# Attention over turned probabilities with the values as weights, and a turned gate, in block 2 of a two-block network

## The reference, cut to what matters

```python
hx = rms_norm(xs, norm_g) * (1 + scale_x) + shift_x
px = split_cols(hx @ w_in + b_in)
ya_x = conv_module(*px[0:3], ...)                     # 31 taps, 512 channels
yb_x, yb_c = gla_branch(px[3:9], pc[3:9], ...)        # 4 heads, chunks of 64 tokens
yc_x, yc_c = attn_branch(px[9:13], pc[9:13], ...)
xs = xs + gate_x * (merge of sigmoid(p13)*ya, sigmoid(p14)*yb, sigmoid(p15)*yc) @ w_out

def gqa_attend(q, k, v):          # 8 query heads, 2 key heads, 64 columns a head
    s = einsum('bqkgd,bskd->bkgqs', q, k) * 64 ** -0.5
    p = softmax(s, axis=-1)
    return einsum('bkgqs,bskd->bqkgd', p, v)
# attn_branch: y = (gqa_attend(...) * silu(gate)) @ w_o; latent queries see context and latent keys
# gla: o_t = q_t S_t, S_t = diag(a_t) S_{t-1} + k_t^T v_t, forward and backward; y = (rms_norm(o) * silu(gate)) @ w_o
```

## Time and profile before

| what | value |
|---|---|
| median of 3 runs | 1383.57 us (1382.19 to 1385.09) |
| the profiled execution's own time | 1383.59 us |
| its span | 1382.3 us |
| mean granted clock | 0.965 |
| TensorE busy | 1310.0 us, 95% |
| VectorE busy | 874.7 us, 63% |
| ScalarE busy | 592.0 us, 43% |
| GpSimd busy | 283.6 us, 21% |
| bytes moved | 168.18 MB |

### The profile page before, as it was taken

One profiled execution on the slowest core, in us unless ns is written; L12 is line 12 of the kernel. 1 busy time (PEld: TensorE's weight loads), 2 busy tenths in 40 slices (PEclk: granted clock), 3 DMA queues, 4 the chain that ended last, 5 costly groups with the idle time before them and its releaser, 6 DMA issues.

```text
span 1382.3 us, 19655 instructions
## 1 busy us (share of the span) xinstructions
PE 1310.0 (95%) x7838; PEld 1057.4 (77%) x7838; DVE 874.7 (63%) x1514; ACT 592.0 (43%) x985; POOL 283.6 (21%) x225
## 2 busy tenths in 40 slices
PE   7999987999979899997999999999999998899998
PEld 5777776777757777776677788888898877579997
DVE  4795766685577643488998542233776677745555
ACT  3444533344453454322433552243563554336543
POOL 0110012210033321136200011111452141300222
PEclk9999998999999999999999999999999998879999
DMA  7683465363433511112111122222653332204453
GB/s 252 224 268 134 151 244 181 126 242 138 145 114 99 162 55 60 46 62 77 61 50 57 61 62 91 92 92 92 200 166 97 107 107 77 76 31 138 131 180 117
DMA packets 49142, 168.18 MB, mean 122 GB/s; under 512 B 5844, under 2 KB 7060, under 8 KB 48794
## 3 DMA queue, kind: packets, MB, share of 16 engines
q1 hardware_dynamic: 49050, 166.92, 36.5%
HBM read 165.85 MB, written 1.05 MB: 121 GB/s over the span
## 4 chain that ended last, share of the span: by engine, by line
PE 78%; DVE 8%; issue 8%; POOL 4%; ACT 1%; DMA 1%; SPq 0%; POOLq 0%; ACTq 0%; DVEq 0%
PE bank L1533 10%; PE bank L1534 9%; PE bank L1535 9%; PE bank L1551 8%; PE bank L1552 7%; PE bank L1553 7%; PE bank L1460 4%; PE bank L1868 3%; PE bank L1573 2%; PE bank L1574 2%; PE bank L1575 2%; DVE conv_val L2630 2%; DVE w_lo L2310 2%; PE bank L1635 2%; PE bank L1843 2%
## 5 line engine op out<-in xcount | busy, mean ns | idle before, releaser
L2310 DVE TENSOR_TENSOR w_lo<-w_raw,w_hi 128x1024 fp32r<-128x1024 f32 (+3 forms) x264 | 324.6, 1233 | 219.8 <-ACT w_hi L1905 219.4
L1905 ACT ACTIVATE w_hi<-w_raw 128x1024 fp32r<-128x1024 f32 (+3 forms) x264 | 269.9, 1027 | 422.4 <-PE bank L1535 143.3
L1533 PE MATMUL bank<-w_hi,x_hi 128*128 128x512 f32 (+4 forms) x784 | 322.3, 411 | 16.1 <-DVE x_lo L2319 9.9
L1534 PE MATMUL bank<-w_lo,x_hi 128*128 128x512 f32 (+4 forms) x784 | 303.1, 387 | 0.0
L1535 PE MATMUL bank<-w_hi,x_lo 128*128 128x512 f32 (+4 forms) x784 | 302.9, 386 | 0.0
L1551 PE MATMUL bank<-x_hi,w_hi 128*128 128x512 f32 (+1 forms) x576 | 204.0, 354 | 0.5 <-ACT conv_val L2105 0.4
L1552 PE MATMUL bank<-x_hi,w_lo 128*128 128x512 f32 (+1 forms) x576 | 196.9, 342 | 0.0
L1553 PE MATMUL bank<-x_lo,w_hi 128*128 128x512 f32 (+1 forms) x576 | 196.6, 341 | 0.0
L1533 PEld LDWEIGHTS bank<-w_hi,x_hi 128*128 128x128 f32 x784 | 151.6, 193 | 55.0 <-DVE x_lo L2319 12.0
L1535 PEld LDWEIGHTS bank<-w_hi,x_lo 128*128 128x128 f32 x784 | 150.3, 192 | 31.2
L1534 PEld LDWEIGHTS bank<-w_lo,x_hi 128*128 128x128 f32 x784 | 151.1, 193 | 25.8
(11 more groups left out here) (349 smaller groups left out, 1906.9 us busy)
## 6 DMA issues: line engine op xcount, KB each, us to landing
w_raw<-in_w SPq DMA_DIRECT2D x172, 512.0 KB, 3.6
w_raw<-in_wm SPq DMA_DIRECT2D x48, 512.0 KB, 4.9
w_raw<-in_wo SPq DMA_DIRECT2D x40, 512.0 KB, 3.7
w_raw<-in_wy_gla SPq DMA_DIRECT2D x8, 512.0 KB, 3.6
w_raw<-in_wy_att SPq DMA_DIRECT2D x8, 512.0 KB, 3.5
w_raw<-in_wy_conv SPq DMA_DIRECT2D x8, 512.0 KB, 3.6
w_raw<-in_w SPq DMA_DIRECT2D x8, 460.0 KB, 4.5
w_raw<-in_w SPq DMA_DIRECT2D x12, 288.0 KB, 2.8
```

The costliest lines, as they stand in the source:

```text
L1533: mm(out, xh[:, q, col], hi[:, kk, 0:w], start=kp == 0 and kk == 0 and not with_bias, stop=False)
L1534: mm(out, xh[:, q, col], lo[:, kk, 0:w], start=False, stop=False)
L1905: do(hi, raw, ACT.Copy).then_inc(sem["cut_hi"], 1)
L2310: v.tensor_tensor(lo, raw, hi.bitcast(F32), ALU.subtract).then_inc(sem["cut_lo"], 1)
```

## The change

Values become the weight in `a_v`, turned probabilities move, and two heads (one of each key head) lie in two column groups, so that the output comes out turned (channels as rows). `a_v` is one step a pair and waits for both copies. The probabilities are scaled by VectorE in `a_inv`, before the flip, which now waits for it; `att_out2` is a plain copy. The gate of attention is projected turned (`project_t` and the new `ev_ag`, with the bias among the parameters); it is kept in `e3` (layer 0, once the last `gla_con` has read it) or in `acc` (layer 1). `y2_gate` (GpSimd) multiplies, for 128 channels and all tokens at a time, `y2_hi` (ScalarE) and `y2_lo` (VectorE) cut; the flips of `y2` go. In `gla_o` the matmuls of both row groups alternate.

```diff
-            yield from inp(AG, tiles, gated)
+            yield from project_t(l, AG)
...
+        elif i == 2:
+            for j in range(4):
+                yield [("y2_gate", l, j), ("y2_hi", l, j), ("y2_lo", l, j)]
...
-        values = lambda i: iter([[("a_v", l, qt, j)] for j in pair(i)])
+        values = lambda i: iter([[("a_v", l, qt, i)]])
...
-    "a_flip": lambda l, qt, j: [("a_exp", l, qt, j)],
+    "a_flip": lambda l, qt, j: [("a_inv", l, qt, j)],
-    "a_v": lambda l, qt, j: [("a_t_act", l, qt, j), ("a_t_dve", l, qt, j), ("ev2", l, KKV, 3)],
+    "a_v": lambda l, qt, i: [("a_t_dve", l, qt, 2 * i), ("a_t_act", l, qt, 2 * i + 1), ("ev2", l, KKV, 3)],
+    "ev_ag": lambda l, j: [("project_t", l, AG, NP - 1, j), ("mi_x", l, 3) if l == LAYERS - 1 else ("gla_con", l, 0, 3, 1)],
+    "y2_gate": lambda l, j: [("ev_ag", l, j)] + [("att_out2", l, t) for t in tiles_of(l)],
+    "y2_hi": lambda l, j: [("y2_gate", l, j)] + before_flip(l, 2),
+    "y2_lo": lambda l, j: [("y2_hi", l, j)],
-    "gla_e": lambda l, t: [*BLOCK1_OVER, ("gla_z", l, t)],
+    "gla_e": lambda l, t: [*BLOCK1_OVER, ("gla_z", l, t), ("y2_gate", l - 1, 3)],
...
     def gla_o(l, t):
...
-        for h in range(HEADS2):
-            par, pair = h % 2, h // 2
-            for d in range(2):
-                mm(bk, b.att[:, i, par, 2 * d + pair, :], b.gv[:, t, h * P:(h + 1) * P], start=d == 0, stop=False)
+        for pair in range(2):
+            part = [k.bank[ps][:, pair * P:(pair + 1) * P] for ps in (even, odd)]
             for d in range(2):
+                for par in range(2):
+                    h = 2 * pair + par
+                    mm(part[par], b.att[:, i, par, 2 * d + pair, :], b.gv[:, t, h * P:(h + 1) * P], start=d == 0, stop=False)
+            for d in range(2):
                 for half in range(2):
...
-                    ins = mm(bk[hs, :], b.q_t[rows, 2 * d + pair, i, hs], b.st[rows, d, pair, step, :],
-                             start=False, stop=d == 1)
+                    for par in range(2):
+                        rows = slice(par * HD, (par + 1) * HD)
+                        ins = mm(part[par][hs, :], b.q_t[rows, 2 * d + pair, i, hs], b.st[rows, d, pair, step, :],
+                                 start=False, stop=d == 1)
...
     def a_v(l, qt, pair):
...
-                ins = mm(k.bank[i][:, at * HD:(at + 1) * HD], turned[:, (g * nb + c) // 2, (g * nb + c) % 2 * P:((g * nb + c) % 2 + 1) * P],
-                         b.kkv[:, t, QK2 + P + kh * HD:QK2 + P + (kh + 1) * HD], start=c == 0, stop=c == nb - 1)
+                for kh in range(2):
+                    j, n = 2 * pair + kh, g * nb + c
+                    at = places(qt, j)[g] // 2
+                    ins = mm(k.bank[i][kh * HD:(kh + 1) * HD, at * P:(at + 1) * P],
+                             b.kkv[:, t, QK2 + P + kh * HD:QK2 + P + (kh + 1) * HD],
+                             k.turned_home(l, qt, j)[:, n // 2, n % 2 * P:(n % 2 + 1) * P],
+                             start=c == 0, stop=c == nb - 1, tile_position=(0, kh * HD))
...
+    def ev_ag(l, j):
+        do(k.turned_gate(l, j), ps[:, 0:n_tok], ACT.Silu, bias=b.par[:, l, AG_BIAS + j:AG_BIAS + j + 1]).then_inc(sem["ev_ag"], 1)
...
     def a_inv(l, qt, j):
...
-        v.reciprocal(stat[:, 2 * AH + at[0]:2 * AH + at[-1] + 1:2], stat[:, AH + at[0]:AH + at[-1] + 1:2]).then_inc(sem["a_inv"], 1)
+        one = dve.own(v.reciprocal(stat[:, 2 * AH + at[0]:2 * AH + at[-1] + 1:2], stat[:, AH + at[0]:AH + at[-1] + 1:2]))
+        dve.wait_ge("own", one)
+        for g in range(n_maps):
+            part = prob[:, g * halves:(g + 1) * halves, :]
+            ins = v.tensor_scalar(part, part, stat[:, 2 * AH + at[g]:2 * AH + at[g] + 1], None, ALU.mult)
+        ins.then_inc(sem["a_inv"], 1)
...
     def att_out2(l, qt):
...
-        v.tensor_tensor(pairs(b.aq[:, qt, :]), pairs(ps[:, :]),
-                        inv.rearrange("p (a b) -> p a b", b=2).unsqueeze(3).to_broadcast([P, AH // 2, 2, HD]),
-                        ALU.mult).then_inc(sem["att_out2"], 1)
+        v.tensor_copy(b.aq[:, qt, :], ps[:, :]).then_inc(sem["att_out2"], 1)
...
+    def y2_gate(l, j):
+        g.tensor_tensor(part, part, k.turned_gate(l, j).rearrange("p (t q) -> p t q", q=P), ALU.mult).then_inc(sem["y2_gate"], 1)
```

More of the change, by code:

```diff
@@ L376, in second_main @@
             yield from project_t(l, CGATE)
-        elif i == 2 and not gates_kept(l, AG):
-            yield from inp(AG, tiles, gated)
+        elif i == 2 and l < LAYERS - 1:
+            yield from project_t(l, AG)
         yield from project_t(l, first)
-        if i == BRANCHES[l][0] and gates_kept(l, AG):
-            yield from inp(AG, tiles, gated)
+        if i == BRANCHES[l][0] and l == LAYERS - 1:
+            yield from project_t(l, AG)
         yield from project_y(f"y{i}", l, 0)
@@ L389, in branch_operands @@
     for i in BRANCHES[l]:
-        if i > 0:
-            c = (None, GG, AG)[i]
+        if i == 1:
             for t in tiles_of(l):
-                yield ([("gated", l, c, t)] if gates_kept(l, c) else []) + flip(f"y{i}", l, t, 0)
+                yield [("gated", l, GG, t)] + flip("y1", l, t, 0)
+        elif i == 2:
+            for j in range(4):
+                yield [("y2_gate", l, j), ("y2_hi", l, j), ("y2_lo", l, j)]
 def merged(l):
@@ L604, in after @@
             return [("cut_lo", self.piece_of[kind, l, c, kp])] + (
-                [("conv_lo", l, 2 * kp + 1)] if kind == "y0" else [("flip_lo", kind, l, t, 0) for t in tiles_of(l)])
+                [("conv_lo", l, 2 * kp + 1)] if kind == "y0" else [("y2_lo", l, 2 * kp + 1)] if kind == "y2" else
+                [("flip_lo", kind, l, t, 0) for t in tiles_of(l)])
         return AFTER[stage](*step[1:]) if stage in AFTER else []
@@ L1155, in emptied @@
     elif stage == "a_v":
-        out.append(("a_prob_t",) + key)
+        out += [("a_prob_t", key[0], key[1], 2 * key[2] + half) for half in range(2)]
     elif stage == "gate_ones":
@@ L1495, in flip @@
         else:
-            pe.wait_ge("gated", l, GG if source == "y1" else AG, t)
+            pe.wait_ge("gated", l, GG, t)
         pe.wait_ge(*(before or ()))
@@ L1564, in project_y @@
             pe.wait_ge("conv_lo", l, 2 * kp + 1)
+        elif kind == "y2":
+            pe.wait_ge("y2_lo", l, 2 * kp + 1)
         else:
@@ L2193, in gla_e @@
             block1_over(act)
+        else:
+            act.wait_ge("y2_gate", l - 1, 3)
         one = act.own(do(e3, ps[:, :], ACT.Abs))
@@ L2954, in gated @@
     def gated(l, c, t):
-        o = b.gv if c == GG else b.aq
         pool.wait_ge("ev_gate", l, c, t)
-        pool.wait_ge("gla_n" if c == GG else "att_out2", l, t)
-        g.tensor_tensor(o[:, t, :], o[:, t, :], k.gate_home(l, c, t), ALU.mult).then_inc(sem["gated"], 1)
+        pool.wait_ge("gla_n", l, t)
+        g.tensor_tensor(b.gv[:, t, :], b.gv[:, t, :], k.gate_home(l, t), ALU.mult).then_inc(sem["gated"], 1)
+    def y2_gate(l, j):
+        part = k.attended(l, j)
+        pool.wait_ge("ev_ag", l, j)
+        for t in tiles_of(l):
+            pool.wait_ge("att_out2", l, t)
+        g.tensor_tensor(part, part, k.turned_gate(l, j).rearrange("p (t q) -> p t q", q=P), ALU.mult).then_inc(sem["y2_gate"], 1)
     def gla_zero(l):
```

132 lines of the change are left out of this document (70 added, 62 removed).

## The result

The changed kernel takes 1348.01 us (median of 4 runs, 1346.54 to 1349.63); the kernel before took 1382.88 us beside it. The ratio is 0.9748, with a 95% interval from 0.9727 to 0.9769: 35 us less. The forecast was 1359.4, 24 us less, and its range ended at 1350. Run again on another occasion, the two took 1349.35 and 1383.15 us, 0.9768 (0.9750 to 0.9786).

What follows compares the result with a forecast made beforehand. TensorE, busy for 95% of the span, was taken as the bound, so matmuls saved in block 2 were mostly time saved. 12.8 + 1.4 + 9 + 1.3 - 0.2 + 2.3 - 2.4 = 24.2 us off 1383.6 gave 1359.4, range 1350 to 1373.

Steps and rivals of the forecast that it cites:

- part 3: Attention's gate, projected turned: bias matmuls save 1.3 us, layer 1 projections lose 0.2, dropped y2 flips save 2.3.
- Part 1: Attention's value matmuls: two overlapping column groups, 1.02 us per 16 records; 12.8 us saved at full clock, 1.4 at half.
- Part 2: Matmul order inside the gated linear attention's output: a tile falls from 4.8 to 3.4 us, 9 us saved over six.
- Part 4: Scaling of probabilities on VectorE: 25 us added there, mostly covered; four maps without cover lose 2.4 us.
- The cover: Projections queued on TensorE between attention steps hide the scaling in 680 to 840 and 1240 to 1295 us: no loss.
- Rival A: Value matmuls' column groups don't overlap: that saving becomes -2 instead of 14.2 us, total 1375.6; chance 0.08.
- Rival B: VectorE becomes the bound between 680 and 760 us; 8 us of layer 0 given back, 1367; chance 0.17.
- Rival C: Clock stays up in 1200 to 1225 us, as the output before it is quicker; 1353 us; chance 0.15.
- Rival D: VectorE's in-order queue: taps ahead of scalings delay flips 1.5 us for each of 40 maps; 1417 us; chance 0.05.
- Rival E: Saving is given back at TensorE's two waits, whose ends hang on GpSimd and VectorE; about 1383 us; chance 0.05.

Runs made afterwards that it cites:

- before_pad: Kernel before with 32 bytes per partition of unused SBUF ahead of everything allocated after the parameters; 1370.06 us, ratio 0.9906.
- after_pad: Kernel after with 224 bytes per partition of unused SBUF behind the parameters, so what follows lies where it lay before; 1358.73 us, ratio 0.9819.
- the two experiments: New gated linear attention output order put into the kernel before (1376.15 us, ratio 0.9947); old order put back into the kernel after (1359.63 us, 0.9821).
- no_scaling: Kernel after without the 48 scaling products on VectorE and the wait behind the reciprocal; 1355.25 us, ratio 0.9796.
- one_group: Kernel after with both heads' value matmuls sent to the first column group, adding up there; 1368.84 us, ratio 0.9881.
- order_only: Kernel before with only the new order of matmuls inside the gated linear attention's output; 1376.15 us, ratio 0.9947.

## Why the prediction was right and wrong

**What it missed.** The step that failed is in part 3: "No weight DMA moves; the bias loads shrink." The edit to the parameters and the selector was costed by its transfers alone, as nothing. It also moves every tensor behind them, and that was worth 7 to 10 us to the kernel after (7.1 by the ratios and in block 2, 9.4 by the medians, 9.8 against the ratio of the first measurement) and 11 to 13 us to the kernel before (before_pad). 1359.4 less 7 to 10 is 1349 to 1352; the measured 1348.0 and 1349.4 lie just beyond the range's end at 1350, and without the move the kernel takes 1358.73, 0.7 us from the forecast. That this is so close is partly luck, as the terms show.

The prediction also named a sign of its own failing, waits of TensorE that grow by more than 5 us in all, and that sign came: they grow by 5.8 us in the table below, and by 7.0 from the profile of before to that of after. It had only 2.4 for them.

**The terms,** with the placement held fixed. The spacings between successive starts on TensorE, added up by kind of matmul over the profiles of before (the second one) and after_pad; the waits are those between the first and the last matmul:

| term | forecast, us | before | after_pad | difference |
|---|---|---|---|---|
| values | -14.2 | 38.4 | 22.1 | -16.2 |
| gated linear attention's output | -9.0 | 28.9 | 20.0 | -8.9 |
| flips of `y2` | -2.3 | 5.3 | 3.0 | -2.3 |
| projections, output products and bias | -1.1 | | | -0.9 |
| all other matmuls | 0 | | | -1.9 |
| TensorE waits | +2.4 | 62.2 | 68.1 | +5.8 |
| sum | -24.2 | | | -24.4 |

- Part 1: a pair at 1.02 us was right to the hundredth, and came from the tiled row of the right width. The 2.0 us beyond the forecast come mostly from the two groups at half clock, which saved 3.3 us (2 x 3.47 to 1.90 and 1.78) and not 1.4: half had been taken off because TensorE waits around them. The other 18 saved 13.0; they took 1.75 us on average before and not 1.83, since some came in two halves of 0.81. The 0.1 for leaving the mode was too much: the four transposes behind a value group take 0.41 us (681.54 to 681.95 in the timeline) where others take 0.36 (683.42 to 683.78), 0.05 more. The Trainium skill ("TensorEngine Tiling (Array Packing)", Key Properties) says that a change of mode drains the array; the trace agrees that there is a cost, and it is of that size.
- Part 2: 3.26 us a tile against 3.4 forecast; the matmuls are 8.9 us less, and the two experiments lie on either side of the 9 us (7.3 and 10.3), since waits change too.
- Part 3: the flips and the projections came as forecast.
- Part 4: 0.49 us for a scaling against 0.48; 15.7 of the 25 us lie in layer 0, not 17. The cover held in layer 0, and in layer 1 the scaling cost 1.2 us, not 2.4 (no_scaling).
- The waits: in block 2 they grew from 23.5 to 30.4 us (after_pad), 4.3 of it in layer 1's attention (8.2 to 12.6), of which the scaling explains 1.1. By TensorE's waits there in after, 2.1 us is one wait for ScalarE's `conv_u` and 1.5 lie ahead of the gated linear attention's output, and neither is in before. That they came with the new order of steps is likely, but no run shows it. The prediction's sum had nothing for them ("waits of a few us may move").
- Rival A fell by one_group. Rival B did not happen, but was one product a map away. Rival C's mechanism happened: matmul time at half clock fell from 72 to 58 us over the whole kernel, which is some 7 us less work time, of which the forecast had 1.4; the half clock within layer 1's attention went from 23.9 to 13.7 us. It wasn't the quicker output that did it, as C had said, for order_only still has 27.3 us there. The longer waits ate most of that. So the sum of -24.4 is closer to -24.2 than its parts are. Rival D fell: TensorE doesn't wait at all from 670 to 800 us in the kernel after. Rival E fell by the time.

## What to carry to other kernels

Matmuls with 64 output rows each, put in turn into two column groups, took 1.02 us for 16 records where one group took 1.90. Matmuls of 64 by 64 in two row groups took half the time when the issue order alternated between the groups (0.60 us for 16, where the earlier trace rows have 0.59 for 8), and that loop order alone was worth 0.5% to 0.8% of this kernel. For column groups no run tried another order. An edit that changes the size of any tensor moves all that is allocated behind it: compare against the old kernel with the old addresses restored by padding before you credit the edit. And where one engine covers another, double the covered work once: it tells how much cover is left, which leaving it out does not.

## What the runs showed of the hardware

The distance between the stationary and the moving operand in SBUF changes the spacing of cut float32 matmuls of 512 columns between 228 and 234 ns and of 256 columns between 116 and 120 ns (means at full clock, eight placements in steps of 32 bytes), in opposite directions in some placements. Over this kernel that is up to 13 us, 1%.

Two of the 48 scalings took 1.26 and 1.58 us in place of 0.49. The timeline of the kernel after, in layer 1, VectorE and GpSimd:

```profile
1173.80 1.27 POOL L2995 TENSOR_TENSOR gla_v<-gla_v,merged 128x512 f32<-128x512 f32 x1 [1.42 <-DVE gla_v L2779]
...
1174.10 1.26 DVE L2851 TENSOR_SCALAR lent_prob<-lent_prob,att_stat 128x512 f32<-128x512 f32 x1
...
1179.83 0.49 DVE L2851 TENSOR_SCALAR lent_prob<-lent_prob,att_stat 128x512 f32<-128x512 f32 x1
...
1180.15 1.30 POOL L3046 TENSOR_TENSOR gla_v<-gla_v,rows 128x512 f32<-128x512 f32 x1
...
1182.28 1.58 DVE L2851 TENSOR_SCALAR att_p<-att_p,att_stat 128x512 f32<-128x512 f32 x1
...
1182.31 1.26 POOL L2995 TENSOR_TENSOR gla_v<-gla_v,merged 128x512 f32<-128x512 f32 x1 [0.87 <-DVE gla_v L2779]
```

Both of the long ones ran while GpSimd worked on a product of 512 columns, and ended 0.3 us behind it. The one at 1179.83 took its 0.49: a GpSimd operation of 4 columns ran beside it, and a product of 512 columns began only 0.32 us into it. The Trainium skill ("SBUF — State Buffer", Who interferes with whom) says that VectorE, in its two-port modes, and GpSimd contend for a shared pair of ports under an exclusive lock, and that whichever issues first blocks the other for a whole instruction. The trace agrees, with 1.26 and 1.58 us in place of 0.49, and here it was VectorE that was held up. In the second case VectorE's record starts 0.03 us ahead of GpSimd's, so the recorded order of starts doesn't tell which one is held up. The forecast had looked only at GpSimd being locked out between 680 and 760 us, and not at VectorE in layer 1, where these two fell into the stretch in which TensorE had nothing else queued. Together they are 1.9 us late. no_scaling took them away with the other 46, and TensorE's waits in that attention fell by 1.1 us: that bounds what they cost here.
